# Attention scores of two heads on both row halves, rotations moved into later steps, and a final stage by halves

## The chip, the cores and the metric

One core of a Trainium2 chip runs one program. TensorE multiplies matrices, VectorE and ScalarE work on tiles of 128 partitions, GpSimd adds sums of squares and makes some low parts, and SyncE issues most DMAs. The metric is the device time of one execution in microseconds; the kernel before took 1373.84 us, the median of 3 runs (1373.65 to 1375.49).

## The reference

Two transformer blocks follow each other on x of 512 rows (tokens) and 1024 columns, all in float32. What matters here:

```python
# first block
h = rms_norm(x, norm_mix_pre)
qa, ka, va, qb, kb, vb = split(h @ w_in)          # 8 q heads, 2 k, 2 v heads of 64, twice
out_a = global_attention(rope(rms_norm(qa)), rope(rms_norm(ka)), va)
out_b = window_attention(rope(qb), rope(kb), vb, sink)   # |key - query| <= 128
x = x + rms_norm(concat(rms_norm(out_a), rms_norm(out_b)) @ w_out)
x = x + rms_norm(silu_ffn(rms_norm(x)))
# second block: pooling and stick-breaking attention, merged, an ffn, and at the end
gate = sigmoid(rms_norm(x, norm_ple) @ w_ple_gate)
x = x + gate * (p @ w_ple_proj)
return rms_norm(x, norm_final)
```

## The kernel before

The activations stand transposed, feature by token: a tile of 128 features by 512 tokens is a chunk, and x is eight chunks (KD). Every float32 operand is split into a high part (type fp32r) and a low part, and a product is three fp32r matmuls: high by high, low by high, high by low. Weights come as units of 128x2048 (sixteen 128x128 tiles), 117 of them, through three slots: ScalarE makes w_hi, VectorE w_lo (`split`, L862 and L1257). TensorE is written out by hand in program order; the engines are tied by semaphores only, and each engine executes its own list in order.

**Input projection ("in1").** Twelve chunks in the order ORDER1 = [5, 4, 0, 10, 1, 2, 6, 3, 7, 8, 9, 11]: 5 and 11 are V of the two head groups (a and b), 4 and 10 their keys, 0 to 3 and 6 to 9 the queries, two heads of 64 rows in each chunk. ScalarE evacuates each to a slot of y (three slots, taken in turn; `evacuate` waits for the slot's last reader). TensorE multiplies it with a rotation matrix, and for group a with a matrix that sums squares per head (`item`, called beside the following chunk); VectorE's `rope(j)` makes the rotated and normed chunk; ScalarE copies each head's 64 rows to the high part (`high_qk`), and GpSimd subtracts to get the low part (`low_qk`, L450, L451, L454). A head's high and low q lie on the two row halves of one tile, so that a matmul of 128 rows takes both; k is held in copies on both halves. Chunks with position below LATE1 = 9 in ORDER1 are rotated during in1; position 9, 10 and 11 in attention steps 1, 5 and 9 (rotations on VectorE at steps 3 and 7).

**Attention.** 64 steps, a head h and a block b of 128 queries each (STEPS); the first 32 look at all 512 keys (group a), the last 32 at two or three blocks of keys, with a sink and masks (group b). Head is the outer index: all four blocks of a head, then the next head. In a step s, TensorE issues scores(s + 2), from step 10 on, at even steps, a part of `weighted` (probabilities by V, a column-tiled pair of fp32 matmuls for two heads), and then the transposes of step s (L675), which wait for VectorE's normalisation (pn_ready). VectorE: reciprocal, normalisation (L1261), `negmax(s + 2)` (L1430). ScalarE: exponential, and `copy_pt(s - 2)` of the transposes. Scores use banks s % 3, and a score is

```python
for part in range(2):
    last = mm(ps[:, bank, at:at + w], q[:, h, b * P:(b + 1) * P], k[:, part, h // 4, k0 * P:k1 * P], ...)
```

A weight unit is split at step 17 (VectorE) and 16 (ScalarE). From step 44 (NORM_A_STEP) the group norm of group a runs beside the steps.

**Tail ("pleg").** Eight gate chunks, 24 matmuls of 512 columns each. Per chunk VectorE scales it (`gate_in`), ScalarE takes the sigmoid, VectorE multiplies by PP and adds to X, ScalarE squares, GpSimd adds to sqsum. `gate_in(j + 1)` stands ahead of the rest of chunk j on VectorE. After the last: sums by column matmuls (`total`), variance, guess (after a table load), refinement, diagonals, factor matmul, eight OUT operations (L1264) and eight stores of 256 KB, one per chunk, each issued as soon as its chunk is ready.

## Time and profile before

| what | value |
|---|---|
| median of 3 runs | 1373.84 us (1373.65 to 1375.49) |
| profiled execution | 1378.3 us, its span 1376.5 us |
| TensorE busy (matmuls) | 1329.5 us, 97% of the span |
| VectorE busy | 694.8 us, 50% |
| ScalarE busy | 546.1 us, 40% |
| GpSimd busy | 150.3 us, 11% |
| stores of the result | 8 of 256 KB, 2.0 us from issue to landing |

Ends of matmuls are modelled, so the distance from start to start tells more than a matmul's duration. "Idle before" in brackets is the engine's idle time ahead of an instruction with what ended it. An attention step is found in the trace by its transposes (ps<-ident,F): four of them in each of the first 32 steps, two or three in the others. In this execution the first scores start at 99.1 us, the transposes of step 10 at 122.45, of step 28 at 151.47, of step 32 at 157.37 and of step 62 at 206.6; the output projection starts at 210.4.

### The profile page before, as it was taken

To read this page: it belongs to the slowest core of one execution; us is meant where nothing else is said; L and a number is where in the kernel's file an instruction comes from. 1 tells how busy PE (TensorE), PEld (TensorE's weight loads), DVE (VectorE), ACT (ScalarE), POOL (GpSimd) and SP (SyncE) were. 2 spreads that over 40 slices of the span, in tenths; PEclk is the share of its full clock that TensorE was granted. 3 is DMA by queue.
4 is the path that set the end of the run, shared out by engine and by line. 5 is a ranking of instruction groups with operands and counts; after the bars stand their busy time and mean duration, and the time that the engine had idled before them with its cause. 6 is when DMAs were issued, how large, how long until landed. Compare 5 with 4: busy or idle time off the path is not lost.

```text
span 1376.5 us, 14683 instructions
## 1 busy us (share of the span) xinstructions
PE 1329.5 (97%) x6056; PEld 1066.9 (78%) x6056; DVE 694.8 (50%) x907; ACT 546.1 (40%) x733; POOL 150.3 (11%) x136
## 2 busy tenths in 40 slices
PE   7987989999999999999999999999999999999995
PEld 5764657888888888887888777888888888888874
DVE  6998773665444442126534455563544354423254
ACT  6558864543233222225224555542423232222232
POOL 3351012510000000103000001012000000010021
PEclk9999989999999999999999999999999999999997
DMA  6110003122222222331321111233222223232311
GB/s 242 62 61 1 1 1 122 63 92 95 106 105 92 92 75 94 105 96 66 130 92 62 62 62 64 90 99 115 94 92 92 92 94 107 69 105 92 117 62 61
DMA packets 20594, 117.74 MB, mean 86 GB/s; under 512 B 2480, under 2 KB 2864, under 8 KB 9904
## 3 DMA queue, kind: packets, MB, share of 16 engines
q1 hardware_dynamic: 19680, 114.79, 23.8%
q10 hardware_dynamic: 848, 2.01, 0.4%
q8 instruction: 48, 0.79, 0.2%
q14 instruction: 18, 0.15, 0.0%
HBM read 114.70 MB, written 2.10 MB: 85 GB/s over the span
## 4 chain that ended last, share of the span: by engine, by line
PE 89%; DVE 7%; DMA 1%; ACT 1%; issue 1%; SPq 0%; POOLq 0%; POOL 0%; DVEq 0%
PE ps L474 87%; PE ps L675 2%; DVE rt L1264 1%; DVE w_lo L1257 1%; DMA w_raw<-weights 1%; DVE nmax L1430 1%; DVE F L1261 1%; DVE rt L1257 0%; DVE hf L1257 0%; DVE OUT L1264 0%; DVE h_lo L1264 0%; ACT w_hi L862 0%; DVE y L1257 0%; DVE y L1264 0%; DVE diag L1261 0%
## 5 line engine op out<-in xcount | busy, mean ns | idle before, releaser
L474 PE MATMUL ps<-h_hi,w_hi 128*128 128x512 f32 x1248 | 495.2, 397 | 13.2 <-DVE w_lo L1257 10.6
L474 PE MATMUL ps<-h_lo,w_hi 128*128 128x512 f32 x1248 | 487.4, 391 | 0.0
L474 PE MATMUL ps<-h_hi,w_lo 128*128 128x512 f32 x1248 | 487.2, 390 | 0.0
L1257 DVE TENSOR_TENSOR w_lo<-w_raw,w_hi 128x2048 fp32r<-128x2048 f32 (+2 forms) x117 | 246.4, 2109 | 266.8 <-ACT w_hi L862 266.8
L474 PEld LDWEIGHTS ps<-h_hi,w_hi 128*128 128x128 f32 x1248 | 235.2, 188 | 69.7 <-issue 13.8
L862 ACT ACTIVATE w_hi<-w_raw 128x2048 fp32r<-128x2048 f32 (+2 forms) x117 | 201.1, 1721 | 191.0 <-DMA w_raw<-weights 190.8
L474 PEld LDWEIGHTS ps<-h_lo,w_hi 128*128 128x128 f32 x1248 | 235.3, 189 | 51.0 <-issue 3.1
L474 PEld LDWEIGHTS ps<-h_hi,w_lo 128*128 128x128 f32 x1248 | 235.1, 188 | 49.7
L418 POOL TENSOR_TENSOR sqsum<-sqsum,sq 128x512 f32<-128x512 f32 x66 | 95.6, 1448 | 917.5 <-ACT sq L862 915.9
L474 PE MATMUL ps<-mid_hi,w_hi 128*128 128x512 f32 x352 | 136.9, 389 | 0.0
L474 PE MATMUL ps<-mid_lo,w_hi 128*128 128x512 f32 x352 | 136.9, 389 | 0.0
L474 PE MATMUL ps<-mid_hi,w_lo 128*128 128x512 f32 x352 | 136.9, 389 | 0.0
L1257 DVE TENSOR_TENSOR hf<-ps,factors_sb 128x512 f32<-128x512 f32 x56 | 38.6, 690 | 193.7 <-PE ps L474 193.6
L862 ACT ACTIVATE mid_hi<-hf 128x512 fp32r<-128x512 f32 x44 | 27.8, 633 | 209.8 <-DVE hf L1257 209.8
L474 PEld LDWEIGHTS ps<-mid_lo,w_hi 128*128 128x128 f32 x352 | 66.1, 188 | 13.8
L474 PEld LDWEIGHTS ps<-mid_hi,w_lo 128*128 128x128 f32 x352 | 66.1, 188 | 13.8
L474 PEld LDWEIGHTS ps<-mid_hi,w_hi 128*128 128x128 f32 x352 | 66.1, 188 | 13.5
L862 ACT ACTIVATE sq<-sq 128x512 f32<-128x512 f32 x44 | 27.7, 632 | 91.6 <-DVE sq L1257 91.6
L675 PEld LDWEIGHTS ps<-ident,F 128*128 128x128 f32 x208 | 23.9, 147 | 42.7 <-DVE F L1261 39.9
L862 ACT ACTIVATE h_hi<-X,gain 128x512 fp32r<-128x512 f32 x40 | 28.9, 722 | 61.1 <-DVE X L1257 58.4
L675 PE MATMUL ps<-ident,F 128*128 128x128 f32 x208 | 37.6, 297 | 15.2 <-DVE F L1261 15.0
L1430 DVE TENSOR_REDUCE nmax<-ps 128x1 f32<-128x512 f32 (+2 forms) x64 | 37.5, 587 | 17.9 <-PE ps L474 17.7
(187 smaller groups left out, 1188.0 us busy)
## 6 DMA issues: line engine op xcount, KB each, us to landing
w_raw<-weights SPq DMA_DIRECT2D x81, 1024.0 KB, 4.8
w_raw<-weights SPq DMA_DIRECT2D x32, 704.0 KB, 3.9
out_t<-OUT SPq DMA_DIRECT2D x8, 256.0 KB, 2.0
X<-x_t SPq DMA_DIRECT2D x3, 512.0 KB, 7.4
c<-constants ACTq DMA_DIRECT2D x1, 1280.0 KB, 8.8
w_raw<-weights SPq DMA_DIRECT2D x4, 256.0 KB, 8.4
wp_raw<-weights SPq DMA_DIRECT2D x1, 1024.0 KB, 7.0
X<-x_t SPq DMA_DIRECT2D x2, 256.0 KB, 4.1
```

The lines of the kernel that those rows point to most:

```text
L418: nc.gpsimd.tensor_tensor(sqsum[:, :], sqsum[:, :], sq[:, j % 2, :], ALU.add).then_inc(nm.summed.sem, 1)
L474: return nc.tensor.matmul(out, lhsT, rhs, start=start, stop=stop, skip_group_check=loose)
L675: last = nc.tensor.transpose(ps[:, 3 + s % 2, (kb - k0) * P:(kb - k0 + 1) * P], prob[:, s % 3, (kb - k0) * P:(kb - k0 + 1) * P], ident[:, :])
L862: return nc.scalar.activation(out, in_, func, **kw)
L1257: return nc.vector.tensor_tensor(out, a, b, op)
L1261: else nc.vector.tensor_scalar(out, a, s1, None, op0))
L1264: return nc.vector.scalar_tensor_tensor(out=out, in0=a, scalar=s, in1=b, op0=op0, op1=op1)
L1430: nc.vector.tensor_reduce(nmax[:, s:s + 1], ps[:, s % 3, at:end], AX.X, ALU.max, negate=True).then_inc(nmax_ready, 1)
```

## The change

It has four parts. (1) q and k are laid out with high and low parts as separate full tiles, so that a chunk's two heads stand on the two row halves; the scores of two heads are issued together, six matmuls of 64 rows in three pairs, in four banks. The steps alternate between the two heads of a chunk. (2) y slots are gone: chunks go to tiles that are free until later (PP, sq, hf). Low parts of q and k are made by VectorE, GpSimd makes none. (3) LATE1 is 8; chunks 11, 7, 8 and 9 (positions 11, 8, 9, 10) are transposed or rotated at steps 28, 32, 35 and 38 in place of steps 1, 5 and 9; the weight split goes to steps 42 and 43. (4) The last gate chunk is computed in two halves of 256 tokens, and the final norm, OUT and the stores go by halves: six stores, one of them issued by ScalarE.

```diff
-LATE1 = 9
+LATE1 = 8
+LATE_STEP = {11: 28, 8: 32, 9: 35, 10: 38}
-STEPS = [(0, h, b, 0, NB) for h in range(NH) for b in range(NB)] + [
-    (1, h, b, max(b - 1, 0), min(b + 2, NB)) for h in range(NH) for b in range(NB)]
+STEPS = [(0, 2 * c + n, b, 0, NB) for c in range(NH // 2) for b in range(NB) for n in range(2)] + [
+    (1, 2 * c + n, b, max(b - 1, 0), min(b + 2, NB)) for c in range(NH // 2) for b in range(NB) for n in range(2)]
-            QA = sb("QA", [P, NH, S], f32r, st)
+            QA = sb("QA", [P, 2, NH // 2, S], f32r, st)
-        y_late = [hf[:, 0, :], hf[:, 1, :], sq[:, 0, :]]
+        y_last = [sq[:, 1, :], hf[:, 0, :], hf[:, 1, :], sq[:, 0, :]]
         def y_of(j):
-            return y[:, j % 3, :] if j < LATE1 else y_late[j - LATE1]
+            return PP[:, j, :] if j < KD else y_last[j - KD]
+        STORES = [(0, 0, 4), (0, 4, 8), (1, 0, 3), (1, 3, 5), (1, 5, 7), (1, 7, 8)]
...
             sum_squares(n_mix_pre)
-            for j in range(len(ORDER1)):
-                if ORDER1[j] not in V1:
-                    low_qk(j)
+            pool.wait_ge(hvar_ready, len(NORMED))
...
+            def scores(t):
+                kind, h, b, k0, k1 = STEPS[2 * t]
...
+                if t == 16:
                     pe.wait_ge(v_ready, 2)
...
+                for qp, kp in ((0, 0), (0, 1), (1, 0)):
+                    for n in range(2):
+                        r = slice(HD * n, HD * n + HD)
+                        last = mm(ps[:, (2 * t + n) % 4, at:at + w], q[r, qp, c, b * P:(b + 1) * P],
+                                  k[r, kp, (c // 2 + n) % 2, k0 * P:k1 * P], (qp, kp) == (0, 0),
+                                  kind == 0 and qp == 1, loose=True)
...
             for s, (kind, h, b, k0, k1) in enumerate(STEPS):
-                scores(s + 2)
+                if s % 2 == 0:
+                    scores(s // 2 + 1)
                 if s >= 10 and s % 2 == 0:
                     weighted((s - 10) // 8, (s - 10) % 8 // 2)
-                if s in LATE_STEPS:
-                    item(LATE_STEPS[s])
+                for j, at in LATE_STEP.items():
+                    if s == at:
+                        item(j)
...
+            for i in range(2):                      # last gate chunk, TensorE
+                bank = ps[:, GATE_BANKS[i], half_of(i)]
+                for k in KS:
+                    t = slice((KD + k) * P, (KD + k + 1) * P)
+                    mm(bank, w_hi[slot][:, t], h_hi[:, k, half_of(i)], k == 0, False)
+                    mm(bank, w_hi[slot][:, t], h_lo[:, k, half_of(i)], False, False)
+                    last = mm(bank, w_lo[slot][:, t], h_hi[:, k, half_of(i)], False, k == KD - 1)
+                last.then_inc(half_done, 1)
...
+            square(n_final, KD - 2, X[:, KD - 2, :])      # ScalarE
+            half_gate(0)
+            half_square(0)
+            half_gate(1)
             tables(LN_EXP)
-            guess(n_final)
+            half_square(1)
+            half_guess(0)
+            half_guess(1)
...
+            def low_qk(j):                          # VectorE; called after rope(j + 1) in in1,
+                dve.wait_ge(roped_hi, ROPED.index(c) + 1)      # and two steps after a late rope
...
+                    lo, hi = q[:, 1, i, :], q[:, 0, i, :]
+                low(lo, y_of(j), hi).then_inc(rope_done, 1)
...
+                for j, at in LATE_STEP.items():
+                    if s == at + 1:
+                        rope(j)
+                    if s == at + 3:
+                        low_qk(j)
-                if s == 17:
+                if s == 43:
                     split(UNITS_IN1 + 1)
...
+            for i in range(2):                      # tail, VectorE
+                half_gate_in(i)
+                half_gate_out(i)
+            half_variance(0)
+            half_variance(1)
+            half_factors(0)
+            half_factors(1)
+            half_apply(0, 0, KD)
+            half_apply(1, 0, KD)
```

## Rows read from the trace of the kernel before

**Rows 1.** The page, chain that ended last, share of the span by line.
```profile
PE ps L474 87%; PE ps L675 2%; DVE rt L1264 1%; DVE w_lo L1257 1%; DMA w_raw<-weights 1%; DVE nmax L1430 1%; DVE F L1261 1%; DVE rt L1257 0%; DVE hf L1257 0%; DVE OUT L1264 0%; DVE h_lo L1264 0%; ACT w_hi L862 0%; DVE y L1257 0%; DVE y L1264 0%; DVE diag L1261 0%
```
**Rows 2.** Busy time by stretch: us, each engine (x instructions), PEclk, DMA, GB/s.
```profile
99.10:122.40 23.30, 16.60 (x79) 10.36 (x77) 20.38 (x43) 17.18 (x40) 8.67 (x7) 0.93 0.00 0
122.40:157.30 34.90, 33.03 (x183) 18.75 (x181) 28.49 (x74) 30.47 (x74) 0.00 (x0) 1.00 0.01 1
157.30:169.70 12.40, 12.40 (x82) 8.10 (x80) 9.36 (x40) 10.27 (x32) 0.00 (x0) 1.00 0.00 0
169.70:206.60 36.90, 30.29 (x177) 21.56 (x175) 27.74 (x95) 24.45 (x73) 4.34 (x4) 0.86 0.01 1
210.40:1350.60 1140.20, 1135.91 (x5140) 933.83 (x5139) 513.84 (x553) 401.34 (x422) 93.40 (x92) 1.00 0.26 90
```
**Rows 3.** Timeline of VectorE, projection: start us, us, what, [idle before <-releaser].
```profile
22.29 2.29 DVE L1257 TENSOR_TENSOR w_lo<-w_raw,w_hi 128x2048 fp32r<-128x2048 f32 x1 [0.26 <-ACT w_hi L862]
...
38.37 0.69 DVE L1264 SCALAR_TENSOR_TENSOR rt<-ps,sqsum 128x512 f32<-128x512 f32 x1
...
44.05 0.69 DVE L1264 SCALAR_TENSOR_TENSOR rt<-ps,sqsum 128x512 f32<-128x512 f32 x1
...
82.53 3.38 DVE L1257 TENSOR_TENSOR w_lo<-w_raw,w_hi 128x2048 fp32r<-128x2048 f32 x1
```
**Rows 4.** Timeline of GpSimd at that last one.
```profile
80.79 2.96 POOL L454 TENSOR_TENSOR QA<-y,QA 64x512 fp32r<-64x512 f32 x2 [2.81 <-ACT QA L862]
```
**Rows 5.** Timeline of TensorE in the projection, where it waits.
```profile
71.07 1.10 PE L474 MATMUL ps<-y,c 128*128 128x512 f32 x2 [1.29 <-ACT y L862]
...
80.04 1.12 PE L474 MATMUL ps<-ysq,c 128*128 128x512 f32 x2 [1.82 <-DVE y L1264]
81.00 1.02 PE L474 MATMUL ps<-y,c 128*128 128x512 f32 x2
```
**Rows 6.** Timeline of VectorE at attention step 3.
```profile
106.39 0.68 DVE L1430 TENSOR_REDUCE nmax<-ps 128x1 f32<-128x512 f32 x1
106.99 0.68 DVE L1264 SCALAR_TENSOR_TENSOR F<-hf,c 128x512 f32<-128x512 f32 x1
...
108.92 0.15 DVE L1441 RECIPROCAL rden<-den 128x1 f32<-128x1 f32 x1
...
109.51 0.68 DVE L1430 TENSOR_REDUCE nmax<-ps 128x1 f32<-128x512 f32 x1
```
**Rows 7.** Timeline of TensorE at the same place.
```profile
109.65 0.66 PE L675 MATMUL ps<-ident,F 128*128 128x128 f32 x4 [2.00 <-DVE F L1261]
```
**Rows 8.** Busy time by stretch, the four us after that.
```profile
110.00:114.00 4.00, 4.00 (x14) 2.44 (x13) 2.70 (x6) 2.95 (x7) 2.41 (x2) 0.59 0.00 0
```
**Rows 9.** Timeline of TensorE, one pair of steps.
```profile
121.44 1.08 PE L474 MATMUL ps<-PT,VA 128*64 128x512 f32 x4
122.45 0.66 PE L675 MATMUL ps<-ident,F 128*128 128x128 f32 x4
...
123.41 0.60 PE L675 MATMUL ps<-ident,F 128*128 128x128 f32 x4
...
124.39 0.65 PE L474 MATMUL ps<-PT,VA 128*64 128x512 f32 x2
```
**Rows 10.** Busy time of the second block's score matmuls of 64 rows.
```profile
725.80:728.16 2.36, 2.35 (x16) 1.00 0.48 135
```
**Rows 11.** Timeline of ScalarE, V of group b.
```profile
123.64 1.14 ACT L862 ACTIVATE VB<-ps,stat 128x128 f32<-128x128 f32 x4
```
**Rows 12.** Timeline of all engines, tail.
```profile
1356.26 0.69 DVE L1257 TENSOR_TENSOR hf<-ps,factors_sb 128x512 f32<-128x512 f32 x1 [3.42 <-PE ps L474]
...
1359.01 1.71 POOL L418 TENSOR_TENSOR sqsum<-sqsum,sq 128x512 f32<-128x512 f32 x1 [4.14 <-ACT sq L862]
...
1360.28 1.28 ACT L877 ACT_TABLE_LOAD   x1
...
1368.69 5.36 DVE L1264 SCALAR_TENSOR_TENSOR OUT<-X,gain,ps 128x512 f32<-128x512 f32 x8 [2.17 <-PE ps L474]
```

## What the change is predicted to do

> **What bounds the kernel now.** I read the chain of waits first, then a table of stretches, then each engine's timeline where TensorE is idle. The chain is TensorE matmuls for 87% of the span [rows 1]. The table of stretches shows where it is not: from 210.4 us to 1350.6 us TensorE is busy 1135.9 of 1140.2 us, so nothing touched by this change can shorten that part, and whatever it saves ahead of it shifts the rest as a block. Idle stand the projection before 99.1, the first ten of 64 attention steps (16.6 of 23.3 us busy), the last twenty (30.3 of 36.9), and the tail [rows 2]. In the middle steps TensorE has no slack: 33.0 of 34.9 and 12.4 of 12.4 us.
>
> The executions: the profiled one took 1378.3 us (span 1376.5), 4.5 above the median of 1373.84. All terms are differences of a few us in the profiled execution; I subtract them from the median, the 0.3% between the two being far below their own doubt.
>
> **1. Projection.** GpSimd makes the low parts of q and k, and while it does, VectorE is slow: a 128x2048 subtraction is 2.29 us at 22.29 and 3.38 us at 82.53, under a GpSimd subtraction that began at 80.79 [rows 3, 4]. TensorE then waits 1.29 us for an evacuation to a y slot that GpSimd has not freed and 1.82 us for a rotated chunk [rows 5]. The change gives each chunk its own slot and moves the low parts to VectorE, where nothing of GpSimd's runs beside them. Laid out by undisturbed durations, VectorE has from 38.37 us on five normed rotations (5.68 each, 38.37 to 44.05), two plain ones (1.93, as at 106.99), four w_lo (2.29), two table scalings (1.3 together), five q chunks' low parts and two keys' of three operations each (11 x 0.64): 49.8 us [rows 3, 6]. It is through at 88.2, well before TensorE, whose own work now ends the stage. Gain: 1.29 + 1.82, the 0.9 of chunk 8's rotation matmul that leaves the stage (one such takes 0.96 with the change to it, 80.04 to 81.00 [rows 5]), and 0.6, my estimate, of lags beside these two waits: **-4.6**, first scores at 94.5. Bounds: -0.9 (only the moved matmul) and -5.5.
>
> The Trainium skill ("Advanced Engine Details and Errata", the section on VectorE's performance modes) has GpSimd and two-port VectorE operations share the second SBUF port and block each other. By its letter a two-input subtraction, which is in no such mode, would not be slowed, and only the y slot's 1.29 and the moved 0.9 would be gained, 2.2 us; the trace shows 3.38 against 2.29 us for just such a subtraction [rows 3], so the row decides.
>
> **2. Steps 0 to 9.** Before, 99.1 to 122.4 us: 23.3. Two rotations run inside them, each holding VectorE from 106.99 to 108.92, 1.93 us, and TensorE stands 2.00 us [rows 6, 7]; after one follows a stretch at granted clock 0.59 [rows 8], between the levels 1.2 and 2.4 GHz. After, no rotation stands there. VectorE per step: maximum 0.60 (106.39 to 106.99), reciprocal and normalisation 0.59 (108.92 to 109.51) [rows 6]: 2.4 us a pair of steps. Now the scores of both steps come from one batch, after the transposes of the odd step: counted from that step's normalisation, 0.5 us to the end of transposes, three passes and the last one's drain 0.9, landing 0.1: 1.5, against 1.2 that VectorE has to do; then maximum, normalisation, 1.2: a loop of 2.7 us. Start: 3.2 us from first score to first transpose before, 3.5 now, the batch being longer. 3.5 + 5 x 2.7 = 17.0: **-6.3** (bounds -8.5 at 2.4 a pair, -1 if the granted clock falls twice and pairs take 3.2).
>
> **3. Steps 10 to 27.** A pair before is 2.95 us, start to start: outputs 1.01, transposes and scores 0.96, and again 0.98 [rows 9]. Joined scores are three passes of two 64-row matmuls for four of 128 rows. That a pair on the two row halves runs at once is shown in this trace for fp32: 16 records of 64 rows, 1280 columns for each of two heads, in 2.36 us [rows 10]; these are five matmuls of 512 columns, and one after the other, at 0.96 each with a change of shape or 0.86 without, they would be 4.3 to 4.8. No row shows fp32r at 64 rows; I take it to do the same. A pass of 512 columns is 0.227 us (24 of them a chunk; 5140 records of all kinds take 1135.9 us, 0.22 each [rows 2]). Before, 0.96 + 0.98 hold four; now three, and one change of shape of about 0.1 less: 1.94 - 0.23 - 0.1 = 1.61, to 1.72 if the change stays; with 1.01, 2.62 to 2.73. VectorE's loop of 2.7 lies as high, so I take 2.78. Nine pairs: 25.0 for 29.0, of which 2.1 is the w_lo split at step 17 that moves to step 43: **-4.0**. If the halves don't overlap: three passes more, 0.68 a pair.
>
> The skill ("TensorEngine Tiling (Array Packing)", Key Properties) says that changing the tiling mode drains TensorE; that speaks against more shapes. The trace prices it: the column-tiled outputs take 1.01 us [rows 9] where two fp32 record times make 0.86, so 0.15 at most for going in and out. The joined scores add a shape of their own, but stand in one block instead of two; by the rule at that price a pair would be 0.15 longer than 2.62, inside the value taken.
>
> **4. Steps 28 to 41.** Here everything that left parts 1 and 2 lands. Step 30: the first windowed scores wait for V of the second group, four scaled copies on ScalarE (1.14 us [rows 11]) behind an exponential and a copy; the scores come 1.6 us late, VectorE's next maximum behind them: +1.6. Steps 33, 36, 39: a rotation (1.93) each, with a 0.86 us matmul ahead of it, and steps 35, 38, 41 a low part (0.6): 7.6 us of VectorE. Windowed pairs took 12.4 us for five and a bit [rows 2] with VectorE busy 9.4, 3.0 idle: 7.6 - 3.0 = +4.6. Shorter scores before and between: -0.4. **+5.8** (bounds: +3 if all idle time is usable; +9 with two stretches at half clock, 1.6 each).
>
> **5. Steps 42 to 63.** The split arrives, +2.1, on ScalarE first and VectorE a step later. Joined windowed scores save TensorE 0.35 a pair, but TensorE is idle here for 6.6 of 36.9 us [rows 2] and at 0.86 clock: I count 2.6 of 3.5. **-0.5** (bounds +3, -4).
>
> **6. Tail.** Before, the last evacuation starts at 1356.26. Then VectorE does chunk 6's product after chunk 7's evacuation, the last GpSimd addition ends at 1360.72, ScalarE loads a table from 1360.28, OUT runs from 1368.69 to 1374.05, and the span ends 2.45 later [rows 12]. After: chunk 6 is finished first, by 1354.2. Half 0 is complete from 1353.7 and goes through at some 0.4 us an operation (0.69 for a whole one; bounds 0.35 and 0.69). Half 1 ends at 1356.3 (48 matmuls of 256 columns, 0.12 each: +0.2); evacuation, sigmoid, product, sum until 1357.9; but the table load, 1.28, stands ahead of its square: 1358.4, square 1358.8; its two sums and their landing 1359.5. GpSimd's last addition now ends at 1356.2 and is off the chain, and so are the sixteen records of sums but four. Variance and guess 1360.2; VectorE refines and makes diagonals for both halves 1359.7 to 1361.9; 16 half operations of OUT at 0.39: 1368.1. Last store 2.45 after that, 1370.6. The stores' rows are 1 KB instead of 2; before, 2.1 MB left in 5.3 us of OUT. Same rate for the low bound, half the rate (10.5 us from 1364) for the high: ends 1370.5 and 1374.7; I add 0.4: 1371.0. **-5.5** (bounds -1.8, -6.5).
>
> Sum: -4.6 - 6.3 - 4.0 + 5.8 - 0.5 - 5.5 = -15.1; 1373.84 - 15.1 = 1358.7.
>
> **Rivals.** (a) The row halves don't run at once in fp32r. For: no such row. Against: [rows 10]. Full pairs 16 x 0.68 = 10.9, windowed 16 x 0.35 less what idle time hides, 2.5: +13.4, 1372. The skill ("TensorE: Matmul & The Clock Gate", the section on packing small matmuls) measured 3.07 for four row tiles; at three quarters of the ideal a pass would be 0.07 longer, some +3 over all, inside the forecast's range. (b) TensorE's clock falls more often: steps 0 to 9 and 28 to 63 leave it busy two thirds, and before it went to 0.59 after a 2.00 us wait [rows 7, 8]. Each fall costs 1.6 us; four more, +6.4: 1365. (c) The tail's halves gain little, because stores or half operations at full length bind: 1362. (d) Slower: the steps from 28 on go at the low clock for most of the time, since three rotations and a split in 16 steps keep opening waits of 2 us. Those steps hold 40 us of TensorE work; all at 1.2 GHz would be +40 less 15 of idle time: 1384. It turns the sign from 60% of them; against it, a slow stretch makes TensorE busy, and each one before lasted 3 us.
>
> **How the numbers follow.** Forecast 0.64; (a) 0.05; (b) 0.17; (c) 0.10; (d) 0.04. 1353 to 1366 holds the forecast with its bounds, (b) and (c). A measurement can tell 0.2%, 2.7 us: faster takes the first four cases nearly whole, 0.95; same 0.01; slower 0.04.
>
> **What would show it.** First scores at 94.5 us and no GpSimd work between 22 and the first squares of group a; step 10's transposes at 111; pairs of 2.7 to 2.8 us with six 64-row records in 0.9 us (1.4 would be (a)); TensorE waits of about 2 us at the three rotations and nowhere earlier; end of steps 9 to 11 us earlier; last OUT some 12 us after the last gate matmul instead of 18. Wrong if the attention ends less than 5 us earlier, or if the stores run on after OUT for more than 3.5 us.

## Result and the profile after

The changed kernel took 1379.55 us (median of 20 runs, 1377.48 to 1389.78), the kernel before, run beside it, 1376.66 us (20 runs, 1373.65 to 1378.9): ratio 1.0025, 95% interval 1.0016 to 1.0035. Forecast were 1358.7 us; the change made the kernel slower by 0.25%. The profiled execution has a span of 1376.8 us (before 1376.5).

Where it went, by the starts of the same landmarks in both traces (first score, transposes of steps 10, 28, 42 and 62, first matmul of the output projection, last gate matmul, end):

| stretch, us | before | after | difference | predicted |
|---|---|---|---|---|
| to the first score | 99.1 | 93.3 | -5.8 | -4.6 |
| steps 0 to 9 | 23.3 | 21.3 | -2.0 | -6.3 |
| steps 10 to 27 | 29.0 | 26.9 | -2.1 | -4.0 |
| steps 28 to 41 | 18.2 | 29.1 | +10.9 | +5.8 |
| step 42 to the output projection | 40.8 | 44.8 | +4.0 | -0.5 |
| from there to the end | 1166.1 | 1161.5 | -4.6 | -5.5 |

The two ends went nearly as predicted. The attention between them, which was to gain 5.0 us, took 10.8 us more. Its stretches in the table of windows of the changed kernel (us, busy time of PE, PEld, DVE, ACT and POOL with instructions, PEclk, DMA share, GB/s), the first, second and fourth of which answer to the first three lines and the fourth of [rows 2]:

```profile
93.30:114.60 21.30, 17.39 (x88) 9.98 (x87) 14.75 (x37) 14.53 (x36) 0.00 (x0) 0.76 0.00 0
114.60:141.50 26.90, 26.90 (x169) 14.19 (x168) 22.25 (x58) 23.69 (x58) 0.00 (x0) 1.00 0.01 2
141.50:170.50 29.00, 25.14 (x140) 13.11 (x138) 21.00 (x65) 17.47 (x48) 0.00 (x0) 0.94 0.00 1
170.50:210.70 40.20, 33.58 (x192) 20.17 (x190) 29.63 (x94) 25.48 (x76) 5.74 (x4) 0.83 0.00 1
215.40:1356.00 1140.60, 1136.30 (x5143) 934.20 (x5143) 513.98 (x554) 401.36 (x421) 92.65 (x91) 1.00 0.27 90
```

Two things are to be seen. In the second line TensorE is busy without a gap, although it has one pass (a run of 512 columns through TensorE) less to do in each pair of steps. And the granted clock is 0.76 in the first line and 0.83 in the fourth: between the first score and the output projection the trace has 27.3 us at the 1.2 GHz level, in five stretches, where before has 13.7 us in four. These are single executions, and the low clock comes and goes between them: the changed kernel's steps 0 to 9 stand unchanged in e3_v20, e7_win128 and e10_high_later below, whose traces have no low clock there, where this one has 10.2 us.

The pair of steps that answers to [rows 9], timeline of TensorE:

```profile
117.51 1.10 PE L669 MATMUL ps<-ident,F 128*128 128x128 f32 x8
118.53 0.96 PE L464 MATMUL ps<-KA,QA 64*128 64x512 f32 x6
119.43 1.08 PE L464 MATMUL ps<-PT,VA 128*64 128x512 f32 x4
120.44 0.33 PE L669 MATMUL ps<-ident,F 128*128 128x128 f32 x1
```

Six score matmuls of 512 columns in 0.90 us, start to start: the two row halves do run at once, and rival (a) falls. But eight transposes take 1.02 us, where twice four of them and the scores took 0.96 and 0.98 before, so the pair is 1.02 + 0.90 + 1.01 = 2.93 us, against 2.95.

The first windowed scores (issued at step 30), where TensorE waits 1.49 us for the scaled copies of V and VectorE's next maximum comes 2.34 us after its last work; and one of the three late rotations, for which ScalarE waits 2.39 us with an exponential queued behind it:

```profile
142.60 1.14 ACT L886 ACTIVATE VB<-ps,stat 128x128 f32<-128x128 f32 x4
143.99 0.61 PE L464 MATMUL ps<-KB,QB 64*128 64x256 f32 x6 [1.49 <-ACT VB L886]
145.01 0.42 DVE L1493 TENSOR_REDUCE nmax<-ps 128x1 f32<-128x257 f32 x1 [2.34 <-PE ps L464]
...
158.39 0.63 ACT L886 ACTIVATE QB<-hf 128x512 fp32r<-128x512 f32 x1 [2.39 <-DVE hf L1299]
158.93 0.46 ACT L886 ACTIVATE F<-ps,nmax 128x257 f32<-128x257 f32 x1
```

The weight split at steps 42 and 43, same view: ScalarE's next exponential stands behind its 1.94 us, then VectorE's next step behind w_lo. GpSimd's addition of squares begins inside w_lo, which is not slowed by it (2.28 us); the normalisation that begins while it runs takes 1.17 us, where the same size took 0.42 at 171.62.

```profile
168.83 1.94 ACT L886 ACTIVATE w_hi<-w_raw 128x2048 fp32r<-128x2048 f32 x1
170.63 0.61 ACT L886 ACTIVATE F<-ps,nmax 128x385 f32<-128x385 f32 x1
...
171.62 0.42 DVE L1303 TENSOR_SCALAR F<-F,rden 128x384 f32<-128x384 f32 x1
...
172.42 2.28 DVE L1299 TENSOR_TENSOR w_lo<-w_raw,w_hi 128x2048 fp32r<-128x2048 f32 x1
...
173.15 4.09 POOL L439 TENSOR_TENSOR sqsum<-sqsum,sq 128x512 f32<-128x512 f32 x2 [94.33 <-ACT sq L886]
...
174.87 1.17 DVE L1303 TENSOR_SCALAR F<-F,rden 128x384 f32<-128x384 f32 x1
```

The tail, which answers to [rows 12]: the additions of GpSimd are off the chain, the table load still stands ahead of the last square, OUT ends at 1373.96 us, 12.5 us after the end of the last gate matmul.

```profile
1361.17 0.28 PE L464 MATMUL ps<-h_hi,w_lo 128*128 128x256 f32 x1
...
1362.75 1.28 ACT L901 ACT_TABLE_LOAD   x1
...
1364.05 0.42 ACT L886 ACTIVATE sq<-X 128x256 f32<-128x256 f32 x1
...
1367.61 6.35 DVE L1306 SCALAR_TENSOR_TENSOR OUT<-X,gain,ps 128x256 f32<-128x256 f32 x16 [0.34 <-PE ps L464]
```

### The profile page after: what moved, and what is told of

It is laid out like the page before. It is cut to its first block, busy times and chain, and to the rows that moved or that the text cites. A ratio compares the mean times of both kernels' runs of the same rounds, so it can differ in the third digit from the quotient of the medians.

```text
span 1376.8 us, 14823 instructions
## 1 busy us (share of the span) xinstructions
PE 1336.7 (97%) x6146; PEld 1065.0 (77%) x6146; DVE 687.8 (50%) x936; ACT 539.7 (39%) x727; POOL 115.6 (8%) x112
## 4 chain that ended last, share of the span: by engine, by line
PE 92%; DVE 4%; ACT 2%; DMA 1%; issue 0%; SPq 0%; DVEq 0%; ACTq 0%
PE ps L464 90%; PE ps L669 2%; DMA w_raw<-weights 1%; DVE w_lo L1299 1%; DVE F L1303 1%; DVE nmax L1493 1%; ACT w_hi L886 0%; DVE OUT L1306 0%; DVE hf L1299 0%; DVE h_lo L1306 0%; DVE X L1299 0%; DVE F L1306 0%; ACT F L886 0%; DVE hf L1306 0%; ACT hf L886 0%
## 5 line engine op out<-in xcount | busy, mean ns | idle before, releaser
L464 PE MATMUL ps<-h_hi,w_hi 128*128 128x512 f32 (+1 forms) x1256 | 495.9, 395 | 13.0 <-DVE w_lo L1299 10.4
L464 PE MATMUL ps<-h_hi,w_lo 128*128 128x512 f32 (+1 forms) x1256 | 488.6, 389 | 0.0
L464 PE MATMUL ps<-h_lo,w_hi 128*128 128x512 f32 (+1 forms) x1256 | 488.4, 389 | 0.0
L1299 DVE TENSOR_TENSOR w_lo<-w_raw,w_hi 128x2048 fp32r<-128x2048 f32 (+2 forms) x117 | 242.0, 2072 | 272.2 <-ACT w_hi L886 272.0
L439 POOL TENSOR_TENSOR sqsum<-sqsum,sq 128x512 f32<-128x512 f32 x66 | 97.2, 1473 | 956.6 <-ACT sq L886 954.7
L1299 DVE TENSOR_TENSOR hf<-ps,factors_sb 128x512 f32<-128x512 f32 (+1 forms) x57 | 38.7, 681 | 190.3 <-PE ps L464 190.1
L464 PEld LDWEIGHTS ps<-mid_hi,w_hi 128*128 128x128 f32 x352 | 66.1, 188 | 13.7
L464 PEld LDWEIGHTS ps<-mid_hi,w_lo 128*128 128x128 f32 x352 | 66.1, 188 | 13.6
L886 ACT ACTIVATE sq<-sq 128x512 f32<-128x512 f32 x44 | 27.7, 632 | 90.2 <-DVE sq L1299 90.2
L1493 DVE TENSOR_REDUCE nmax<-ps 128x1 f32<-128x512 f32 (+2 forms) x64 | 37.5, 587 | 27.2 <-PE ps L464 27.2
```

The lines of the kernel that those rows point to most:

```text
L439: nc.gpsimd.tensor_tensor(sqsum[:, :], sqsum[:, :], sq[:, j % 2, :], ALU.add).then_inc(nm.summed.sem, 1)
L464: return nc.tensor.matmul(out, lhsT, rhs, start=start, stop=stop, skip_group_check=loose)
L886: return nc.scalar.activation(out, in_, func, **kw)
L1299: return nc.vector.tensor_tensor(out, a, b, op)
L1493: nc.vector.tensor_reduce(nmax[:, s:s + 1], ps[:, s % 4, at:end], AX.X, ALU.max, negate=True).then_inc(nmax_ready, 1)
```

## The experiments

My theory after the result: tail and projection bring what they should; the attention loses it by three parts, the shape changes around 64-row scores, the late V, rotations and split, and a lower granted clock that follows from them. "Ratio" is against runs of the kernel before that were made beside each kernel, with its 95% interval; medians of different rows were taken beside different runs of it (1376.11 to 1376.97 us), so differences between rows under about 2 us are not told apart. "Clock" is the median over the executions of their mean granted clock (for before, of each of the four sets beside the experiments). Stretches are from each kernel's one profiled execution, us; "low" is the time at the 1.2 GHz level from the first score to the output projection.

| kernel | median (runs) | ratio | clock | to 1st score | 0-9 | 10-27 | 28-41 | 42-61 | low |
|---|---|---|---|---|---|---|---|---|---|
| before | 1376.66 (20) | | 0.988-0.990 | 99.1 | 23.3 | 29.0 | 18.2 | 37.0 | 13.7 |
| after | 1379.55 (20) | 1.0025 (1.0016-1.0035) | 0.985 | 93.3 | 21.3 | 26.9 | 29.1 | 40.2 | 27.3 |
| e1_tail | 1371.96 (5) | 0.9963 (0.9951-0.9974) | 0.990 | 99.2 | 23.4 | 29.0 | 18.2 | 35.9 | 13.7 |
| e2_inproj | 1378.82 (12) | 1.0011 (0.9997-1.0026) | 0.985 | 97.2 | 22.3 | 27.2 | 20.4 | 46.1 | 34.1 |
| e3_v20 | 1376.82 (12) | 1.0009 (0.9994-1.0024) | 0.987 | 93.5 | 18.7 | 27.2 | 26.1 | 42.9 | 20.5 |
| e4_rows128 | 1373.08 (8) | 0.9975 (0.9965-0.9985) | 0.991 | 93.5 | 18.9 | 27.1 | 28.3 | 36.9 | 10.2 |
| e5_fill | 1378.11 (12) | 1.0011 (0.9999-1.0023) | 0.990 | 93.7 | 18.7 | 27.2 | 26.6 | 45.5 | 20.5 |
| e6_split17 | 1372.91 (7) | 0.9982 (0.9963-1.0001) | 0.991 | 94.0 | 19.6 | 30.0 | 27.7 | 33.1 | 10.2 |
| e7_win128 | 1371.86 (5) | 0.9970 (0.9958-0.9982) | 0.990 | 93.6 | 18.7 | 27.2 | 25.1 | 36.9 | 6.8 |
| e8_inproj_fill | 1379.72 (12) | 1.0019 (1.0009-1.0029) | 0.990 | 96.5 | 22.6 | 27.2 | 24.8 | 40.7 | 20.5 |
| e9_stacked | 1373.88 (11) | 0.9974 (0.9964-0.9984) | 0.991 | 94.2 | 19.9 | 30.0 | 30.6 | 32.6 | 13.7 |
| e10_high_later | 1375.20 (12) | 0.9989 (0.9974-1.0004) | 0.990 | 92.9 | 18.7 | 30.0 | 26.3 | 36.8 | 10.2 |
| e13_slots | 1372.18 (5) | 0.9966 (0.9954-0.9979) | 0.990 | 99.8 | 23.2 | 29.0 | 18.2 | 33.8 | 6.8 |
| e14_dve_low | 1369.57 (5) | 0.9946 (0.9933-0.9960) | 0.991 | 94.3 | 25.6 | 29.0 | 18.2 | 34.1 | 10.2 |
| e15_inproj_split17 | 1373.66 (9) | 0.9975 (0.9965-0.9985) | 0.988 | 96.6 | 23.8 | 30.1 | 20.4 | 33.1 | 13.7 |
| e16_stacked_pool | 1371.11 (5) | 0.9956 (0.9942-0.9969) | 0.992 | 93.8 | 18.7 | 30.0 | 28.0 | 32.5 | 6.8 |

Executions of one kernel differ by their clock: of e3_v20's twelve, the shortest took 1373.81 us at a mean granted clock of 0.991, the longest 1387.66 at 0.976. So does a stretch of one profiled execution from another's: the code of steps 42 to 61 is the same in before, e1_tail, e13_slots and e14_dve_low, and took 37.0, 35.9, 33.8 and 34.1 us with 10.2, 10.2, 3.4 and 3.4 us of low clock in it.

**The tail alone (e1_tail).** The kernel before with part (4) of the change.

> The kernel before with the change's tail alone (last gate chunk in two halves, norm, OUT and six stores by halves). Theory: the tail is the one part that went as predicted, and it is independent of the attention; last gate matmul to end 15.9 us instead of 21.1, and 0.7 us more from the output projection's start to that matmul, so -4.6 us against before (ratio 0.9967), all of it behind 1350 us. Rival: the gain in the changed kernel needed its earlier steps too (another phase of the weight stream), and alone it is under 2 us.

Measured -4.4 us. From the start of the last gate matmul to the end it is 15.6 us, where before has 20.7 (the expectation has both 0.3 to 0.4 too long). The theory holds.

**The rotations back in the projection (e2_inproj), V earlier (e3_v20).**

```diff
-LATE1 = 8
-LATE_STEP = {11: 28, 8: 32, 9: 35, 10: 38}
+LATE1 = 11                                    # e2_inproj; e3_v20 keeps LATE1 = 8
+LATE_STEP = {11: 20}                          # e3_v20: {11: 20, 8: 32, 9: 35, 10: 38}
```

> The changed kernel with all rotations inside the projection (chunks 7, 8 and 9 rotated there, nothing of them at steps 32 to 41), and V of group b at step 20. Theory (the late rotations and V are what cost 10.9 us in steps 28 to 41): first scores 3 to 4.5 us later than the changed kernel (96.5 to 98), steps 28 to 41 in 21 us instead of 29.1, later steps unchanged; in sum 4 to 5 us below the changed kernel, 1375. Rival (the joined scores and their alternating order cost it, the rotations only stand beside): steps 28 to 41 stay at 26 us or more, and the kernel is no faster than the changed one, about 1380.

> The changed kernel with only V of group b moved from step 28 to step 20. Theory: the 1.5 us wait of TensorE ahead of the first windowed scores goes, and the four transposes and copies fit in full steps at 0.7 us of TensorE: -0.8 to -1.5 us, 1378.4. Rival (something else is late at step 30, the exponentials' order on ScalarE): the wait stays at 1 us or more, and the time is that of the changed kernel or 0.5 us more.

e2_inproj: steps 28 to 41 went from 29.1 to 20.4 us, as the theory said, so the late V and rotations, with the low clock beside them, are most of what made them long. They are not all of it: without V, rotation or low clock the stretch still takes 2.2 us more than before's 18.2, and TensorE is busy in all of it (e15_inproj_split17, same code there):

```profile
150.40:170.80 20.40, 20.40 (x134) 11.70 (x132) 14.18 (x56) 14.80 (x45) 0.00 (x0) 1.00 0.00 1
```

And the sum came out as the rival's: steps 42 to 61 rose to 46.1 us, 27.3 of them at the low clock.

e3_v20: 2.7 us below the changed kernel, more than expected. The wait for V went, as the theory said: the pair from step 28 takes 3.02 us instead of 4.45. The pair from step 30 takes 4.31 us in both and 3.35 in e2_inproj: the 0.97 is the rotation matmul that stands at step 32; and 1.6 us of the stretch's 3.0 are low clock that this execution does not have in its pair from step 36 (5.46 for 7.05). V at its new place costs 0.5 us in the pair from step 18 (as it did in the pair from 26) and 0.4 in the pair from 22. Against e2_inproj, with no low clock in either, the three rotations cost 26.1 - 20.4 = 5.7 us, 1.9 each.

**The shape of the scores (e4_rows128).** The same batch, two matmuls of 128 rows a head:

```diff
-                for qp, kp in ((0, 0), (0, 1), (1, 0)):
-                    for n in range(2):
-                        r = slice(HD * n, HD * n + HD)
-                        last = mm(ps[:, (2 * t + n) % 4, at:at + w], q[r, qp, c, ...], k[r, kp, (c // 2 + n) % 2, ...], ...)
+                for n in range(2):
+                    for part in range(2):
+                        last = mm(ps[:, (2 * t + n) % 4, at:at + w], q[:, part, c, ...], k[:, part, (c // 2 + n) % 2, ...], ...)
```

> The changed kernel with each head's score made by two matmuls of 128 rows again (four a pair, in one batch, no shape of 64 rows), in the changed order of steps; they multiply high by high and low by low rows of both heads, so that the values are not the scores: only the time is meant. Theory (the saved pass of 0.23 us is eaten by going into and out of the 64-row shape): a pair in steps 10 to 27 stays at 2.93 us within 0.1, and the whole kernel within 1.5 us of the changed one. Rival (the joined scores do save, and something else keeps the pair at 2.93): the pair takes 3.1 us and the kernel 4 to 5 us more, 1384.

Timeline of TensorE, e4_rows128, a pair in steps 10 to 27:

```profile
115.41 1.10 PE L668 MATMUL ps<-ident,F 128*128 128x128 f32 x8
116.26 1.17 PE L464 MATMUL ps<-KA,QA 128*128 128x512 f32 x4
117.35 1.08 PE L464 MATMUL ps<-PT,VA 128*64 128x512 f32 x4
118.36 0.33 PE L668 MATMUL ps<-ident,F 128*128 128x128 f32 x1
```

The transposes take 0.85 us here and 1.02 with 64-row scores behind them: the pass saved (1.09 to 0.90) is paid for at the change of shape, 1.94 against 1.92 us for both. Behind the scores the change of shape into the outputs is there in both: four passes take 1.09 us, three take 0.90. That half of the theory holds. The other half does not: the kernel was not the same but 6.5 us below the changed one, at a clock of 0.991 for 0.985; its trace has the gain in steps 42 to 61 (36.9 for 40.2) and 0 to 9, where the changed kernel's trace has 10.2 us of low clock and this one none.

**The price of a change of shape (e11_between, e12_ahead; one run each, 1380.17 and 1380.35 us, read for the pairs alone).** In five pairs one more 128-row matmul, either between the second and third pair of 64-row matmuls, or ahead of all six:

```diff
+                    if kind == 0 and 6 <= t < 11 and (qp, kp) == (0, 1):     # e11_between; e12_ahead: before the loop
+                        mm(ps[:, SIDE_BANK, :], ident_r[:, :], KA[:, 0, 0, :], loose=True)
```

> e3_v20 with one more matmul of 128 rows and 512 columns into an unused bank, in five pairs (scores issued at steps 10 to 18), between the second and the third pair of 64-row score matmuls: two more changes of shape than e12_ahead with the same work. Theory (a change between 64 and 128 rows costs 0.17 to 0.2 us): those pairs take 0.35 to 0.4 us more than in e12_ahead, about 3.5 us. Rival (a change costs 0.1 us or less; the saved pass goes elsewhere): at most 0.2 us more than e12_ahead.

> e3_v20 with the same extra matmul in the same five pairs, ahead of the score matmuls, behind the transposes of 128 rows, so that no change of shape is added. Theory and rival alike: a pair takes 2.93 plus 0.22 us for the matmul, 3.15 us, if TensorE bounds the pair; less, if VectorE does.

Timelines of TensorE, e11_between:

```profile
118.02 0.73 PE L464 MATMUL ps<-KA,QA 64*128 64x512 f32 x4
118.68 0.50 PE L464 MATMUL ps<-KA,ident_r 128*128 128x512 f32 x1
119.10 0.50 PE L464 MATMUL ps<-KA,QA 64*128 64x512 f32 x2
119.53 1.08 PE L464 MATMUL ps<-PT,VA 128*64 128x512 f32 x4
```

and e12_ahead:

```profile
117.93 0.47 PE L464 MATMUL ps<-KA,ident_r 128*128 128x512 f32 x1
118.33 0.96 PE L464 MATMUL ps<-KA,QA 64*128 64x512 f32 x6
119.23 1.08 PE L464 MATMUL ps<-PT,VA 128*64 128x512 f32 x4
```

Four 64-row matmuls (two passes, 0.45 us) last 0.66 until the 128-row one starts; that one lasts 0.42 instead of 0.23. A pair took 3.56 us in e11_between and 3.17 in e12_ahead: 0.39 us for two changes, 0.2 each, as the theory had it; e12_ahead's 3.17 are the 2.93 of e3_v20 and the matmul's own 0.23.

**Keeping TensorE busy (e5_fill, e8_inproj_fill).**

```diff
+                for n in range(1 if s < 10 else 2 if 42 <= s < 48 or s >= 59 else 0):    # e8: 34 <= s < 48
+                    mm(ps[:, SIDE_BANK, :], ident_r[:, :], KA[:, 0, 0, :], loose=True)
                 pe.wait_ge(pn_ready, s + 1)
```

> The changed kernel with V at step 20 (e3_v20), and TensorE kept busy where it waits for VectorE: ahead of the wait for a step's normalisation one matmul of 512 columns into an unused bank in steps 0 to 9, two in steps 42 to 47 and 59 to 63. Theory (the granted clock falls because the joined scores and the long waits leave TensorE idle; each fall costs 1.5 to 3 us): stretches at half clock in steps 0 to 9 and 42 to 48 go, half-clock time in the attention falls from 17 to 20 us to 10 or less, the runs scatter less, median 1373.5 (3 us below e3_v20). Rival (the clock does not hang on idle time here; the fillers only take time ahead of the transposes): half-clock time stays, and 26 fillers at 0.1 to 0.2 us on the path add 2 to 4 us: 1380.

> All rotations in the projection (e2_inproj), and fillers as in e5_fill, in steps 34 to 47 instead of 42 to 47. Theory (e2_inproj saves 8.7 us in steps 28 to 41 and loses it again to 20 us of half clock in steps 42 to 58): with the clock held, steps 42 to 62 in 40 us instead of 46, steps 0 to 9 in 15.6 us, median 1371 to 1373. Rival (the fall of the clock follows from the waits after step 48, where no filler stands): steps 48 to 62 stay at 27 us or more and the median at 1377 or above.

Neither kernel gained, and neither theory nor rival came out whole. e5_fill's trace has the same 20.5 us at the low clock as e3_v20's, in the same three stretches 1.4 us later. But over twelve executions each, the mean granted clock is 0.990 for e3_v20's 0.987, and 0.990 for e2_inproj's 0.985 in e8_inproj_fill, whose trace has 13.6 us of low clock in steps 42 to 61 for 27.3 there, with steps 28 to 41 4.4 us longer. So the matmuls did raise the clock somewhat, and the time that they take on TensorE ate what that gave: the medians, 1.3 and 0.9 us higher, are not told apart from those without them.

**The split and the windowed scores (e6_split17, e7_win128, e9_stacked, e15_inproj_split17).** e6_split17 is e3_v20 with the split at steps 16 (ScalarE) and 17 (VectorE); e15_inproj_split17 is the same edit on e2_inproj. e7_win128 is e3_v20 with the edit of e4_rows128 in the windowed steps (kind 1), whose values are then not the scores; e9_stacked does that as a full computation, and has the early split too.

```diff
-                if s == 42:
+                if s == 16:
                     split(UNITS_IN1 + 1)
```

> The changed kernel with V at step 20 (e3_v20), and the weight split back at steps 16 and 17 in place of 42 and 43. Theory (in full steps it costs its 2.1 us, as before; at 42 it costs 2.6 us at pair 42 and part of pair 44, and starts a fall of the clock): steps 10 to 28 +2.1, steps 42 to 62 -4 to -5, the kernel 2 to 3 us below e3_v20, 1374.5. Rival (a split costs its length anywhere): the kernel the same as e3_v20 within 0.5 us.

> The changed kernel with V at step 20 (e3_v20), and the windowed scores (group b) alone by two matmuls of 128 rows a head, the group a scores joined as changed; the values of group b are not the scores, only the time is meant. Theory (the joined form costs where TensorE waits often: its matmuls keep the granted clock lower): steps 0 to 28 as e3_v20, steps 42 to 62 in 37 us instead of 40 to 42, half-clock time 10 us in place of 20, median 1373.5. Rival (what e4_rows128 gained lies in steps 0 to 9): the kernel within 0.7 us of e3_v20, 1376.8.

> The changed kernel with V at step 20, the weight split at steps 16 and 17, and group b's q and k laid out as before (high and low rows of a head on the two halves of one tile), so that the windowed scores are two matmuls of 128 rows a head; a full computation. Theory (the windowed joined form and the late split cost 5 and 4 us of the changed kernel, independently): median 1368 to 1370, half-clock time in the attention 7 us or less. Rival (both gains are the same one, the clock in steps 42 to 48, and come once): 1372, as e6_split17 and e7_win128 each.

> All rotations in the projection (e2_inproj), and the weight split at steps 16 and 17. Theory (e2_inproj lost its 8.7 us again to the split at 42 and the low clock that followed it): steps 42 to 62 in 34 to 36 us instead of 46, steps 28 to 41 in 20.5, half-clock time in steps 42 to 62 7 us or less in place of 27, median 1370. Rival (the clock falls with the windowed joined scores whatever stands at 42): steps 42 to 62 stay at 40 us or more with 15 us or more of half clock, median 1376.

Steps 42 to 61 in the table of windows (TensorE's busy time first, granted clock third from the end): e3_v20, e7_win128, e6_split17, then e2_inproj and e15_inproj_split17.

```profile
165.50:208.40 42.90, 36.27 (x192) 22.02 (x190) 29.75 (x95) 25.58 (x76) 5.75 (x4) 0.76 0.00 1
```
```profile
164.60:201.50 36.90, 28.80 (x174) 19.87 (x173) 29.59 (x95) 25.63 (x76) 5.74 (x4) 0.91 0.01 1
```
```profile
171.20:204.30 33.10, 29.54 (x192) 17.91 (x190) 26.06 (x92) 24.07 (x72) 4.37 (x4) 0.95 0.00 1
```
```profile
167.20:213.30 46.10, 39.42 (x193) 24.47 (x191) 28.75 (x95) 26.03 (x76) 5.80 (x4) 0.70 0.00 1
```
```profile
170.80:203.90 33.10, 29.56 (x193) 17.77 (x191) 26.02 (x93) 24.02 (x72) 4.34 (x4) 0.95 0.00 1
```

With the late split, the joined windowed scores go with a clock of 0.76 and 0.70 in these stretches; take either away and it is 0.91 or 0.95. The clocks over all executions say the same more surely: 0.985 to 0.987 with both (after, e2_inproj, e3_v20), 0.990 to 0.992 in the experiments without one or both but e15_inproj_split17, which has 0.988 (before itself 0.988 to 0.990). The early split costs 2.8 us in steps 10 to 27 and gives 9.8 (e6_split17) and 13.0 us (e15_inproj_split17) back in these two traces, up to 8.5 and 12 of them low clock (half of the 17.1 and 23.9 us that went). The medians moved by -3.9 and -5.2: e6_split17's trace gives some 3 us of its 9.8 back ahead of step 10 and in steps 28 to 41, beside the 2.8, and e2_inproj's profiled execution stood 2.4 us above its median. e7_win128: -5.0.

Part of that is no clock. In the windowed steps the joined form is the slower one at full clock; from the transposes of step 35 to the outputs, in e3_v20 and then in e7_win128:

```profile
151.06 0.55 PE L669 MATMUL ps<-ident,F 128*128 128x128 f32 x3
151.54 0.62 PE L464 MATMUL ps<-KB,QB 64*128 64x256 f32 x6
152.09 0.44 PE L464 MATMUL ps<-mask_r,ident_r 128*128 128x128 f32 x2
152.46 0.64 PE L464 MATMUL ps<-w_raw,VA 128*64 128x512 f32 x1
```
```profile
150.67 0.55 PE L672 MATMUL ps<-ident,F 128*128 128x128 f32 x3
150.97 0.72 PE L464 MATMUL ps<-KB,QB 128*128 128x256 f32 x4
151.53 0.34 PE L464 MATMUL ps<-mask_r,ident_r 128*128 128x128 f32 x2
151.79 0.64 PE L464 MATMUL ps<-w_raw,VA 128*64 128x512 f32 x1
```

1.40 us against 1.12. The pass saved has 256 columns here, and the masks, matmuls of 128 rows, are one more change of shape: the transposes take 0.48 for 0.30, the scores 0.55 for 0.56, the masks 0.37 for 0.26. The pairs from steps 34 and 40 take 3.76 and 3.72 us joined, 3.48 and 3.50 with 128 rows.

The gains of the early split and of 128 rows did not add up in e9_stacked, 1373.9, nearer to its rival (and 2 us above it): its steps 28 to 41 took 30.6 us.

**Where e9_stacked lost it (e16_stacked_pool); ScalarE's order (e10_high_later).** e16_stacked_pool has the low parts of the three late chunks on GpSimd; e10_high_later is e6_split17 with the high part a step later.

```diff
                     if s == at + 2:
                         finish(j)
+                    if s == at + 3:           # e10_high_later, ScalarE; VectorE's low_qk at + 4
                         high_qk(j)
```

> e9_stacked with the low parts of the three late q chunks made by GpSimd, as before the change. Theory (e9_stacked lost 4 to 5 us in steps 28 to 41, 30.6 against 26, to the two-piece copies and subtractions of the late chunks on ScalarE and VectorE): steps 28 to 41 in 26 to 27 us, median 1370. Rival (the copies on ScalarE, two instead of one, are what is late, or the clock): 30 us again, 1373.9 within 0.7.

> e6_split17 (V at 20, split at 16 and 17) with ScalarE's high part of a late rotated chunk one step later (behind the exponential of step at + 3 in place of at + 2), and the low part on VectorE one step later too. Theory (ScalarE waits 1.5 to 2.4 us for the rotation with the next exponential queued behind it): those gaps on ScalarE go, steps 32 to 41 take 0.5 us less for each of three rotations, 1371.5. Rival (VectorE's own 1.9 us for the rotation holds the loop, the exponential behind it is not late): the same as e6_split17, 1372.9, within 0.5 us.

e16_stacked_pool is 2.8 us below e9_stacked, with steps 28 to 41 at 28.0 instead of 30.6 us, of which up to 1.5 are clock (4.4 us at the low level there, and 1.5): the low parts were part of the loss, and less than the theory had.

e10_high_later is not faster (1375.2 against 1372.9; one of its runs took 7595.45 us, which no profile explains): its pairs from steps 34 and 40 take 3.59 and 3.46 us for 3.75 and 3.72, but the one from 36 takes 6.06 where e3_v20, also without low clock there, has 5.46; steps 42 to 61 were 3.7 us longer, at 6.8 us more of low clock. The exponential behind the rotation was worth 0.2 us in two pairs, not 0.5, and the third lost more than both gained.

**The projection alone (e13_slots, e14_dve_low).** e1_tail, with own slots for the chunks, then also with low parts on VectorE; the attention is that of before.

```diff
-            return y[:, j % 3, :] if j < LATE1 else y_late[j - LATE1]
+            return PP[:, j, :] if j < KD else y_last[j - KD]            # both, with evacuate's wait gone
+                        last = tt(q[o, h, :], t, q[r, h, :].bitcast(f32), ALU.subtract)    # e14_dve_low, VectorE
```

> The kernel before with the tail by halves (e1_tail), and a slot of its own for each rotated chunk, GpSimd still making the low parts. Theory (of the changed kernel's 5.9 us in the projection, the y slots hold the smaller share and the contention with GpSimd the larger): first scores at 97.5 to 98.2 us, attention as before, median 1370.5 (1.3 below e1_tail). Rival (the slots are all of it; GpSimd's subtractions lie beside): first scores at 95 or earlier, median 1368.

> e13_slots with the low parts of the chunks rotated in the projection made by VectorE (12 subtractions of 64 rows for six q chunks, 8 for two keys), those of positions 9 and 10 by GpSimd as before; scores, order of the steps and late steps as before. Theory: first scores at 95 to 96 us (94.5 plus the rotation matmul of position 8, 0.96), the attention as before, so 3 to 4 us below e1_tail, 1368.5. Rival (VectorE with 20 subtractions is late in the stage, where the changed kernel has 11): first scores at 96, but the first transposes 5 us behind them instead of 3.2, median 1371.

The slots alone gave nothing that can be told (1372.2 against 1372.0, first score at 99.8 for 99.2), less than expected. The low parts on VectorE brought the first score to 94.3 us, 5.5 earlier, and the kernel to 1369.57, the fastest of all: 0.54% below before, with runs from 1368.55 to 1369.86. That is 2.6 us less than e13_slots; 2.4 of the 5.5 went again in steps 0 to 9 (25.6 us for 23.2, with 3.4 us more of low clock). Its VectorE is late, as the rival said, but the first transposes come 3.8 us behind the first score, not 5:

```profile
93.09 1.39 DVE L1320 TENSOR_TENSOR QA<-PP,QA 64x512 fp32r<-64x512 f32 x2
94.51 1.39 DVE L1320 TENSOR_TENSOR QB<-sq,QB 64x512 fp32r<-64x512 f32 x2
95.82 0.68 DVE L1514 TENSOR_REDUCE nmax<-ps 128x1 f32<-128x512 f32 x1
```

## Why the prediction was wrong, step by step

- **1, projection: right**, -5.8 for -4.6, just beyond its bound of -5.5. That the low parts on GpSimd were most of it is shown by e13_slots and e14_dve_low; the 1.29 us that I gave to the y slots did not come from slots alone. The Trainium skill ("GPSIMD Engine Reference", Specifications) names contention with VectorE instructions that have two SBUF inputs, and [rows 3] agree, 3.38 against 2.29 us; the section that I weighed in the prediction did not name these.
- **2, steps 0 to 9: wrong, a term left out, the loop mis-sized, and the clock.** Its timeline in e3_v20, which has no low clock there, from one batch's maximum to the next:

```profile
102.52 0.69 DVE L1493 TENSOR_REDUCE nmax<-ps 128x1 f32<-128x512 f32 x1 [0.45 <-PE ps L464]
...
103.32 0.49 DVE L1303 TENSOR_SCALAR F<-F,rden 128x512 f32<-128x512 f32 x1
...
103.86 0.66 PE L669 MATMUL ps<-ident,F 128*128 128x128 f32 x4 [0.80 <-DVE F L1303]
...
104.45 0.96 PE L464 MATMUL ps<-KA,QA 64*128 64x512 f32 x6
...
105.46 0.69 DVE L1493 TENSOR_REDUCE nmax<-ps 128x1 f32<-128x512 f32 x1 [0.46 <-PE ps L464]
```

  Maximum to normalisation 0.80 and on to the transposes 0.54 (I had 1.2 for the two), transposes 0.59 (0.5), scores and landing 1.01 (1.0): 2.93 us a pair, not 2.7. And the sum of five pairs forgot the outputs, which stand for the first time ahead of the transposes of step 10, as `weighted` does from there on:

```profile
110.31 0.97 PE L464 MATMUL ps<-KA,QA 64*128 64x512 f32 x6
111.21 1.08 PE L464 MATMUL ps<-PT,VA 128*64 128x512 f32 x4
112.22 0.99 PE L669 MATMUL ps<-ident,F 128*128 128x128 f32 x7
```

  That is 1.0 us of the 1.7 between 17.0 and e3_v20's 18.7; the loop is most of the rest. The other 2.6 us of the miss in the changed kernel's trace are its 10.2 us at the low clock, where pairs took 4.07 us; they came with this execution, as the same code ran without them in e3_v20, e7_win128 and e10_high_later.
- **3, steps 10 to 27: the mechanism right, the price wrong.** The halves run at once and a pass goes. But I took the changes of shape to come out 0.1 cheaper or the same. A change costs 0.2, and the joined scores add one, from the transposes into 64 rows (1.02 against 0.85 us in e4_rows128), while the one into the outputs stays. The Trainium skill ("TensorEngine Tiling (Array Packing)", Key Properties) has the rule that a switch drains the engine; I took it up and under-priced it. A pair gained 0.02 us, to 2.93 for the 2.78 I took. The -2.1 is the split that left (2.4 us in the pairs from 16 and 18) and 0.2 from nine pairs, less 0.5 for the transposes of V, which fall into the pair from 26.
- **4, steps 28 to 41:** +10.9 for +5.8. By the experiments it is V's wait, 1.4 (4.45 to 3.02 in e3_v20; I had 1.6); three rotations, 5.7 (I had 7.6 less 3.0 of VectorE's idle time, 4.6); low clock, 1.6; and the joined form itself, 2.2, where I had -0.4 (e2_inproj's 20.4 against 18.2). So some of the 7.6 was covered, but less than I took: VectorE was idle there, TensorE was not (12.4 of 12.4 us busy in [rows 2]), and each rotation brings it a matmul of 1 us. The largest failed term is the last: "shorter scores" were longer scores.
- **5, steps 42 to the output projection: the step that failed most by its reasoning**, +4.0 for -0.5. I counted the joined windowed scores as a saving of 0.35 us a pair, 2.6 in all; at full clock they cost 0.22 to 0.28 a pair more than 128 rows, since a pass of 256 columns, 0.11 us, is less than what the shape adds at its two ends, 0.18 and 0.11, and making them 128 rows again gave -5.0 us on the median (e7_win128). The split was taken at its length, 2.1; moving it back to steps 16 and 17, where it costs 2.8, gave -3.9 (e6_split17). In both the clock rose with it, 0.987 to 0.990 and 0.991.
- **6, tail: right**, -5.0 behind the start of the last gate matmul and +0.4 ahead of it, -4.6 for -5.5 (-4.4 alone).

Of the rivals, (b), more time at the low clock, came as well, and in the size that I gave it: 13.6 us more than before, four times the 3.4 us of one fall, priced at 6.4 us. I put it at 0.17 and as a small loss from a gain; by itself it would have left 1365. It met with the failed terms of steps 2 to 5, which took at least 9 us beside it: the attention missed its forecast by 15.8 us, and the low clock can be 6.8 of them.

Taken together, e14_dve_low has the tail and the projection's part and the attention of before: the changed kernel is 10 us above it (1379.55 against 1369.57). The two parts outside the attention gave 7.1 us, and the rearranged attention took 10. By the clocks, 0.985 and 0.991, the changed kernel stands at the 1.2 GHz level for some 16 us more, which is 8 us at most; that is an estimate, 0.006 of 1377 us, twice, and half of it lost if TensorE bounds all of that time.

Open: what lowers the clock. It is shown that 64-row windowed scores and a late split together go with it, and that 512-column matmuls put into the waits raise it and take as much time; why is not shown. Nor is the changed order of the steps tested alone.

## What to carry to other kernels

Price a change of a matmul's shape before joining small matmuls: a pass of 512 columns saved is worth 0.23 us, and every change from one shape to another costs about 0.2; with 256 columns or a matmul of another shape in between, joining loses. Work moved into a stage "with idle time" has to be laid against each engine there: VectorE's idle time hid a quarter of the rotations, 1.9 of 7.6 us, as TensorE had none. Count what each step's list holds at both ends of a stretch: an output left out was 1.0 us. And change the parts that share nothing one at a time: here two of four parts were worth 0.5% and hidden under the others.

## What the runs showed of the hardware

- Two 64-row fp32r matmuls on the two row halves run at once: six of 512 columns in 0.90 us.
- A change between 64-row and 128-row matmuls costs 0.2 us (3.56 us a pair in e11_between against 3.17 in e12_ahead, two changes).
- A two-input VectorE subtraction of 128x2048 was slow when a GpSimd operation with 1.2 us still to go was running as it began, and not when one began inside it: 3.37 to 3.39 us in the four cases beside the low parts of before ([rows 3] has one), 2.28 us in the changed kernel at 172.42 with a GpSimd addition from 173.15, and 2.29 alone.
- The higher granted clock does not go with the higher busy share of TensorE in the records: in e7_win128 TensorE was busy 28.8 of 36.9 us at 0.91, in e3_v20 36.3 of 42.9 us at 0.76. Matmuls last longer at the low level, so the share is also an effect of the clock and tells nothing of its cause.
